# Planned times, queue order and output picking in a decoder kernel that attends over paged K/V

## The chip, the cores and the metric

The kernel runs on one core of a Trainium2 chip. The time is the device time of one execution in microseconds (us); lower is better. Three runs of the kernel before gave 2172.71, 2174.38 and 2177.74 us, median 2174.38 us.

## The reference

One inference step of a two-layer decoder, width 2048, for 256 prompt tokens and for 8 sequences of 8 new tokens that have 2048 past tokens each in a paged K/V cache. Layer A is an RWKV-7 recurrence. Layer B is stick-breaking attention with 16 heads of 128, on K and V that are projected once from the residual stream after layer A:

```python
k_p, v_p = _shared_kv(h_p, kv_norm, w_kv)              # prompt
k_past = cache_k[page_table].reshape(Bs, past_len, 16, 128)   # samples: 8 x 16 pages of 128
h_p = h_p + _sb_mix(rmsnorm(h_p), k_p, v_p, ...)       # causal, 256 x 256 per head
h_s = h_s + _sb_mix(rmsnorm(h_s), k_s_all, v_s_all, ...)
# in a block:  z = q.k * scale + bias;  att = exp(log_sigmoid(z) + sum of log_sigmoid(-z) over later keys)
# o = att @ v;  branch = (o * silu(g)) @ w_o,   q, g = split(rmsnorm(h) @ w_qg)
```

The outputs are the two y tensors, the states and shifts of layer A, and the new K and V.

## The kernel before, in words

Channels lie on the 128 partitions and tokens on the free axis: 320 tokens, 256 of the prompt and 64 of the samples. Every projection weight (2048 x 2048) is read in 16 chunks of 1 MB. A chunk is split into two parts of lower precision (`whi` by ScalarE, L1724, `wlo` by VectorE, L1898) and multiplied in three passes (L2100 to L2102). The program has an opening, mixing projections, the recurrence, and then the trunk (`trunk`), which this case is about.

The trunk computes six projections, 96 chunks: WO, Q, K, V, the gate G2, and BO at the end. Beside them run three kinds of work. **Sample attention** goes over 64 blocks (`NK`), each two pages of K and two of V of one sequence, 4 MB a block: scores (L2126), softplus and running sum, transposes (L2139), and the product with V (L2148), which adds up in `psO` over the 8 blocks of a sequence. **Prompt heads**, 16 of them, need the finished Q, K, V and G2 and read them back from DRAM (L1623 to L1625 and L1636, 128 KB each). **News** is the attention of each sequence to its own 8 new tokens, 8 times (L2185 to L2204), from `kN`, `vS`, `gS`. BO needs all heads and all sequences.

In `psO` the four output groups stand in 32-row lanes: of the 16 heads each is valid in a quarter of the rows. Before, ScalarE copies all 512 columns to SBUF (`osb`, L1800; `osn` for the news, L1841), TensorE multiplies the four 128-column parts with columns of the identity (`pick`, L2161 and L2204, 32 columns each), and VectorE stores them (L1987, L2027).

The order on every engine is fixed when the program is built. Each kind of work is a generator that yields a planned time before each step, and `side_by_side` (L567) always takes the step with the lowest planned time:

```python
CHUNK, SHARED = 7.0, 13.4
BLOCK = 12.0
WINDOW = 32 * CHUNK + GAP
SAMPLE = WINDOW + 8.0
HEADS, HEAD = WINDOW + 48 * SHARED + 4.0, 7.8
NEWS, NEWLY = HEADS + 4.0, 12.0
```

`SHARED` is the planned time of one of the 48 chunks of K, V and G2, during which the blocks run; `HEAD` and `NEWLY` are the planned times of a head and of a sequence's news. These numbers decide only the order; what an engine waits for is decided by semaphores. Block k is planned at `SAMPLE + 12 k` = 242 + 12 k. Put into the formulas, the heads began at 881.2, which is 53.3 blocks after the first one, and the news at 885.2; BO's first chunk is at 1031.6. SyncE's queue (SP) issues all loads of the trunk in one order. A load whose buffer isn't free yet holds up everything behind it: pages of K wait for the scores two blocks back (two buffers), pages of V for the value product three pages back (three buffers), Q, K and V of head h for head h-4, and the gate of head h for `p_y` of head h-6 (six buffers). PE starts the value product of a block (L2148) when both its V pages have landed.

Of the kernel before, what the change touches and what calls it, by code (L numbers as in the profile page):

```python
# [18 lines left out]
ALU = mybir.AluOpType  # L19
# [1333 lines left out]
AT_BIASQ, AT_BIAS, AT_MASK = 0, 2, 2 + NHB  # L1353
# [16 lines left out]
CHUNK, SHARED = 7.0, 13.4  # L1370
# [4 lines left out]
HEADS, HEAD = WINDOW + 48 * SHARED + 4.0, 7.8  # L1375
NEWS, NEWLY = HEADS + 4.0, 12.0
# [63 lines left out]
def trunk(nc, c_, a):  # L1440

    with ExitStack() as ctx:
# [11 lines left out]
        st, osb = sb("st", [P, 2, KB, P]), sb("osb", [P, 512])  # L1454
        pt = sb("pt", [1, NB * NPAGE], I32)
        biasQ = c_.consts[:, 3:4]
        pick = c_.ident[:].rearrange("p (g i q) -> p i g q", g=4, i=4)
        with ExitStack() as ring:
# [14 lines left out]
        er, osn = sb("er", [P, P]), sb("o_new", [P, 512])  # L1473
# [21 lines left out]
        att_turned, st_ready = sem("att_turned"), sem("st")  # L1495
# [4 lines left out]
                       (("t", "scored turned valued spread picked"), ("a", "abs exp ln att er st osn"),  # L1500
                        ("v", "z sp rc arg o gate")))
# [20 lines left out]
        def by_lane(x, b):  # L1522
            return x[:, :, TS * b:TS * b + TS].rearrange("p (g i) q -> p i g q", i=4)

        def lanes(x):
            return x.rearrange("p (i g q) -> p i g q", i=4, g=4)
# [19 lines left out]
        def _(sp):  # L1546
# [58 lines left out]
            def news():  # L1605
# [6 lines left out]
                yield HEADS + 16.0  # L1612
# [3 lines left out]
            def heads():  # L1616
                for h in range(NHB):
                    j = h % HRING
                    yield max(head_time(h - HRING, 0.4), low_time(first_chunk(BO) - 1) + 2.7)
# [7 lines left out]
            def gates():  # L1627
                for h in range(NHB):
                    yield max(head_time(h - GRING, 2.3), HEADS + 16.5 if h >= 4 * 3 else HEADS - 1.0)
# [11 lines left out]
            sp.dma_start(c_.consts[:, 2:4], a["at_fixed"][:, AT_BIASQ:AT_BIAS]).then_inc(fixed_in, 16)  # L1641
# [70 lines left out]
        def _(act):  # L1712
# [74 lines left out]
            def turned():  # L1787
                for k in range(NK):
# [19 lines left out]
            def news():  # L1808
# [7 lines left out]
                for b in range(NB):  # L1816
# [75 lines left out]
        def _(dve):  # L1892
# [110 lines left out]
            def news():  # L2003
                for b in range(NB):
# [17 lines left out]
                    Nv.done(dve.tensor_tensor(z_n[:], z_n[:], w_n[:], ALU.subtract), "arg")  # L2022
                    yield new_time(b, 0.86)
# [3 lines left out]
                    Nv.done(dve.tensor_tensor(by_lane(oN, b), lanes(pn_fin), by_lane(gS, b), ALU.mult), "o")  # L2027
                    Nv.wait(dve, "o", b)
                    g = of_sequence(gS, b)
                    Nv.done(dve.tensor_tensor(g, g, pn_er.rearrange("p (h q) -> p h q", q=TS), ALU.mult), "gate")  # L2030
# [48 lines left out]
        def _(pe):  # L2079
# [51 lines left out]
            def turns():  # L2131
                for k in range(NK):
# [20 lines left out]
                    if k % NBLK == NBLK - 1:  # L2153
# [6 lines left out]
                        for i in range(4):  # L2160
                            last = pe.matmul(ps_fin[:, 32 * i:32 * i + 32].rearrange("p (g q) -> p g q", g=4),  # L2161
                                             osb[:, i * P:(i + 1) * P], pick[:, i], start=True, stop=True)
                        last.then_inc(final_summed, 1)

            def news():
                yield NEWS - 5.0
# [8 lines left out]
                for b in range(NB):  # L2175
# [17 lines left out]
                    if b:  # L2193
                        Na.wait(pe, "osn", b - 1)
# [186 lines left out]
```

## Time and profile before

| what | value |
|---|---|
| median of three runs | 2174.38 us |
| the profiled execution: time, span | 2177.72 us, 2176.0 us |
| busy: PE, DVE, ACT, POOL | 89%, 46%, 38%, 12% |
| mean granted clock of TensorE | 0.951 of full speed |
| chain that ended last: PE, DMA | 27%, 20% of the span |
| the largest single item of that chain | landing of V pages, 20% |
| moved by DMA | 508.84 MB |

Times in the rows are microseconds from the start of the span. SPq is the DMA queue of SyncE. In a view by windows, the DMA share is the mean busy share of the core's 16 DMA engines, and PEclk is the granted clock as a share of the full 2.4 GHz. "Idle before, releaser" is the time in which an engine stood still ahead of an instruction, and what ended it.

### The profile page before, as it was taken

Reading aid. Unit: us, or ns where it says so; the run is one execution under the profiler, and the core shown is the slowest. Engines: PE = TensorE matmul, PEld = TensorE weight load, DVE = VectorE, ACT = ScalarE, POOL = GpSimd, SP = SyncE. Lnnn points to the kernel's source line nnn. Section 1 sums busy time; section 2 is a strip of 40 time slices with the busy share of each in tenths; the row PEclk is TensorE's granted clock in tenths of the full one; section 3 lists DMA queues with packets and bytes.
Section 4 is the critical chain, followed back from the end, with each engine's and each line's share of the span. In section 5 each row is a group of like instructions: output and inputs, shape, how many; then the busy total and the mean of one; then the engine's idle time right before and its main releaser. Section 6 shows DMA issues by size and latency. Waiting matters only on the chain.

```text
span 2176.0 us, 49310 instructions
## 1 busy us (share of the span) xinstructions
PE 1938.7 (89%) x20796; PEld 1652.4 (76%) x20796; DVE 993.1 (46%) x1551; ACT 822.9 (38%) x1430; POOL 261.6 (12%) x315
## 2 busy tenths in 40 slices
PE   5799999999799999969999988989988888687797
PEld 3599999999688888869899756656666666344596
DVE  6336364543455555424546433333353333366344
ACT  3523232332455555422323323233233334355332
POOL 2200000000244444313100000000000000010032
PEclk8899999999899999979999999999999999788898
DMA  5455555553222222144564999999999999988441
GB/s 189 155 166 162 176 159 179 168 170 101 76 80 67 74 72 69 46 168 147 222 218 163 419 419 419 418 418 414 410 403 416 419 419 378 343 321 333 157 151 68
DMA packets 119495, 508.84 MB, mean 234 GB/s; under 512 B 19233, under 2 KB 60578, under 8 KB 65826
## 3 DMA queue, kind: packets, MB, share of 16 engines
q1 hardware_dynamic: 119298, 506.00, 61.9%
q8 instruction: 149, 2.44, 0.5%
q14 instruction: 48, 0.39, 0.1%
HBM read 472.33 MB, written 33.63 MB: 233 GB/s over the span
## 4 chain that ended last, share of the span: by engine, by line
PE 27%; DMA 20%; DVE 3%; ACT 2%; SPq 2%; issue 2%; DVEq 0%; ACTq 0%
DMA at_vraw<-in_cache_v 20%; PE psP_ L2100 7%; PE psP_ L2101 6%; PE psP_ L2102 6%; PE at_psO L2148 4%; PE at_psS L2126 2%; DVE wlo_ L1898 1%; SPq L1551 1%; DMA at_gS<-spill_g 1%; DVE resT L2073 0%; SPq L1611 0%; ACT whi_ L1724 0%; ACT at_p_w L1856 0%; DMA wraw_<-in_weights 0%; PE psP_ L2196 0%
## 5 line engine op out<-in xcount | busy, mean ns | idle before, releaser
L2100 PE MATMUL psP_<-xhi,whi_ 128*128 128x320 f32 x1536 | 494.8, 322 | 24.6 <-DVE wlo_ L1898 14.8
L2101 PE MATMUL psP_<-xlo,whi_ 128*128 128x320 f32 x1536 | 478.7, 312 | 0.0
L2102 PE MATMUL psP_<-xhi,wlo_ 128*128 128x320 f32 x1536 | 478.4, 311 | 0.0
L2100 PEld LDWEIGHTS psP_<-xhi,whi_ 128*128 128x128 f32 x1536 | 292.6, 190 | 99.9 <-issue 83.7
L134 PE MATMUL psP<-xhi,whi 128*128 128x320 f32 x1024 | 318.0, 311 | 12.9 <-DVE wlo L169 11.9
L1898 DVE TENSOR_TENSOR wlo_<-wraw_,whi_ 128x2048 fp32r<-128x2048 f32 x96 | 222.1, 2314 | 210.0 <-ACT whi_ L1724 209.2
L135 PE MATMUL psP<-xlo,whi 128*128 128x320 f32 x1024 | 317.1, 310 | 0.0
L136 PE MATMUL psP<-xhi,wlo 128*128 128x320 f32 x1024 | 317.1, 310 | 0.0
L1724 ACT ACTIVATE whi_<-wraw_ 128x2048 fp32r<-128x2048 f32 x96 | 183.5, 1913 | 317.0 <-PE psP_ L2102 311.7
L2101 PEld LDWEIGHTS psP_<-xlo,whi_ 128*128 128x128 f32 x1536 | 293.1, 191 | 0.0
L2102 PEld LDWEIGHTS psP_<-xhi,wlo_ 128*128 128x128 f32 x1536 | 292.4, 190 | 0.0
L169 DVE TENSOR_TENSOR wlo<-wraw,whi 128x2048 fp32r<-128x2048 f32 x64 | 146.7, 2293 | 208.7 <-ACT whi L163 208.7
L2148 PE MATMUL at_psO<-at_vraw,at_st 128*32 128x512 f32 x1024 | 143.9, 686 | 86.1 <-DMA at_vraw<-in_cache_v 80.9
L163 ACT ACTIVATE whi<-wraw 128x2048 fp32r<-128x2048 f32 x64 | 122.3, 1913 | 240.8 <-PE psP L136 237.3
L134 PEld LDWEIGHTS psP<-xhi,whi 128*128 128x128 f32 x1024 | 193.0, 188 | 14.9 <-DVE wlo L169 13.2
L135 PEld LDWEIGHTS psP<-xlo,whi 128*128 128x128 f32 x1024 | 193.1, 189 | 0.0
L136 PEld LDWEIGHTS psP<-xhi,wlo 128*128 128x128 f32 x1024 | 193.0, 188 | 0.0
L2148 PEld LDWEIGHTS at_psO<-at_vraw,at_st 128*32 128x32 f32 x1024 | 29.4, 117 | 147.1 <-DMA at_vraw<-in_cache_v 92.3
L2126 PE MATMUL at_psS<-at_kraw,at_qp 128*32 128x256 f32 x2048 | 128.2, 392 | 0.0
L1793 ACT ACTIVATE at_st<-at_psT 128x256 f32<-128x256 f32 x64 | 24.5, 383 | 249.8 <-PE at_psT L2139 249.7
L2126 PEld LDWEIGHTS at_psS<-at_kraw,at_qp 128*32 128x32 f32 x2048 | 61.3, 112 | 48.1 <-issue 16.4
L1678 POOL COPY at_qp<-at_qS 128x128 f32<-128x128 f32 x8 | 3.2, 412 | 740.8 <-PE at_psS L2126 596.3
(315 smaller groups left out, 2721.7 us busy)
## 6 DMA issues: line engine op xcount, KB each, us to landing
at_kraw<-in_cache_k SPq DMA_DIRECT2D x128, 1024.0 KB, 11.1
at_vraw<-in_cache_v SPq DMA_DIRECT2D x128, 1024.0 KB, 10.9
wraw_<-in_weights SPq DMA_DIRECT2D x96, 1024.0 KB, 6.8
wraw<-in_weights SPq DMA_DIRECT2D x64, 1024.0 KB, 4.9
rw_s0t<-in_s0T SPq DMA_DIRECT2D x16, 256.0 KB, 3.7
o_wkv_s<-rw_SN SPq DMA_DIRECT2D x16, 256.0 KB, 2.3
resT<-in_xT SPq DMA_DIRECT2D x4, 640.0 KB, 5.9
spill_r<-stage SPq DMA_DIRECT2D x4, 640.0 KB, 7.4
```

Source lines behind the costliest of these rows:

```text
L134: pe.matmul(out, wh, c_.xhi[:, kc, :], start=(kc == 0), stop=False)
L135: pe.matmul(out, wh, c_.xlo[:, kc, :], start=False, stop=False)
L136: last = pe.matmul(out, wl, c_.xhi[:, kc, :], start=False, stop=(kc == NM - 1))
L163: act.activation(c_.whi[:, q % 2], c_.wraw[:, q], ACT.Copy).then_inc(c_.whi_ready, 1)
L169: dve.tensor_tensor(c_.wlo[:, q % 2], c_.wraw[:, q], c_.whi[:, q % 2], ALU.subtract).then_inc(c_.wlo_ready, 1)
L1724: act.activation(whi[:, i % 2], wraw[:, q], ACT.Copy).then_inc(c_.whi_ready, 1)
L1898: dve.tensor_tensor(wlo[:, i % 2], wraw[:, q], whi[:, i % 2], ALU.subtract).then_inc(c_.wlo_ready, 1)
L2100: pe.matmul(out, wh, c_.xhi[:, kc, :], start=(kc == 0), stop=False)
L2101: pe.matmul(out, wh, c_.xlo[:, kc, :], start=False, stop=False)
L2102: last = pe.matmul(out, wl, c_.xhi[:, kc, :], start=False, stop=(kc == NM - 1))
L2126: last = pe.matmul(psS[32 * j:32 * j + 32, 0:BK].rearrange("p (t s) -> p t s", t=KB), qp[:, b % 2, j, 32 * i:32 * i + 32], kraw[:, k % KRI ...
L2148: last = pe.matmul(psO[32 * g:32 * g + 32, :], st[:, k % 2, pg, 32 * g:32 * g + 32], vraw[:, (KB * k + pg) % VRING, 512 * g:512 * g + 512] ...
```

## The change

Four things change.

1. **Planned times.** `SHARED` 13.4 to 12.6, `HEAD` 7.8 to 9.6, `NEWLY` 12 to 14, and `NEWS` from `HEADS + 4` to `HEADS + 26`. The heads now begin at 842.8, 50.1 blocks after the first block, and the news at 868.8. The last block and BO keep their planned times.
2. **Queue of loads.** Q, K, V of head h are planned at `head_time(h, -2.6)` and no longer at `head_time(h - 4, 0.4)`; its gate at `head_time(h, -1.2)` and no longer at `head_time(h - 6, 2.3)`. `gS` moves from `HEADS + 16` to `HEADS + 22`.
3. **Picking of outputs.** The four 128-column parts of `psO` (and `psF`) are each multiplied by a 0/1 column of the partitions (`lane(i)`, loaded with the constants) and added up by VectorE in four dependent operations; one transpose on TensorE then gives the result. `osb` and `osn` shrink to 128 columns, ScalarE's copies are gone, and the four products with `pick` become one `transpose`. `oS` and `oN` are stored in plain head order.
4. With these, two waits change their engine: the wait for the last value product of a sequence goes from ScalarE to VectorE, and so does that of the news.

```diff
-AT_BIASQ, AT_BIAS, AT_MASK = 0, 2, 2 + NHB
+AT_BIASQ, AT_LANES, AT_BIAS, AT_MASK = 0, 1, 5, 5 + NHB
-CHUNK, SHARED = 7.0, 13.4
+CHUNK, SHARED = 7.0, 12.6
-HEADS, HEAD = WINDOW + 48 * SHARED + 4.0, 7.8
-NEWS, NEWLY = HEADS + 4.0, 12.0
+HEADS, HEAD = WINDOW + 48 * SHARED + 4.0, 9.6
+NEWS, NEWLY = HEADS + 26.0, 14.0
...
-                yield HEADS + 16.0
+                yield HEADS + 22.0
                 sp.wait_ge(c_.stored, spilled_before(BO))
                 sp.dma_start(gS[:], sample_part("g2")).then_inc(gs_in, 16)
...
-                    yield max(head_time(h - HRING, 0.4), low_time(first_chunk(BO) - 1) + 2.7)
+                    yield max(head_time(h, -2.6), low_time(first_chunk(BO) - 1) + 2.7)
...
-                    yield max(head_time(h - GRING, 2.3), HEADS + 16.5 if h >= 4 * 3 else HEADS - 1.0)
+                    yield max(head_time(h, -1.2), HEADS + 22.0 if h >= 4 * 3 else HEADS - 1.0)
...
-                    if k % NBLK == NBLK - 1:
-                        b = k // NBLK
-                        yield block_time(k, 1.9)
-                        act.wait_ge(valued, KB * (k + 1))
-                        if b:
-                            act.wait_ge(final_summed, b)
-                        act.activation(osb[:], psO[:], ACT.Copy).then_inc(o_copied, 1)
...
-                    yield new_time(b, 0.68)
-                    Nt.wait(act, "valued", b)
-                    if b:
-                        Nt.wait(act, "picked", b - 1)
-                    Na.done(act.activation(osn[:], psF, ACT.Copy), "osn")
...
             def finals():
                 for b in range(NB):
+                    yield block_time(NBLK * b + NBLK - 1, 1.9)
+                    dve.wait_ge(valued, KB * NBLK * (b + 1))
+                    if b:
+                        dve.wait_ge(final_summed, b)
+                    dve.tensor_scalar(osb[:], psO[:, 0:DH], lane(0), None, ALU.mult).then_inc(laned, 1)
+                    for i in range(1, 4):
+                        dve.wait_ge(laned, 3 * b + i)
+                        dve.scalar_tensor_tensor(out=osb[:], in0=psO[:, DH * i:DH * i + DH], scalar=lane(i), in1=osb[:],
+                                                 op0=ALU.mult, op1=ALU.add).then_inc(laned if i < 3 else o_copied, 1)
                     yield block_time(NBLK * b + NBLK - 1, 2.25)
                     dve.wait_ge(final_summed, b + 1)
-                    dve.tensor_copy(by_lane(oS, b), lanes(ps_fin)).then_inc(final_out, 1)
+                    dve.tensor_copy(of_sequence(oS, b), by_head(ps_fin)).then_inc(final_out, 1)
...
+                    yield new_time(b, 0.68)
+                    Nt.wait(dve, "valued", b)
+                    if b:
+                        Nt.wait(dve, "picked", b - 1)
+                    Nv.done(dve.tensor_scalar(osn[:], psF[:, 0:DH], lane(0), None, ALU.mult), "l0")
+                    for i in range(1, 4):
+                        Nv.wait(dve, f"l{i - 1}", b)
+                        Nv.done(dve.scalar_tensor_tensor(out=osn[:], in0=psF[:, DH * i:DH * i + DH], scalar=lane(i),
+                                                         in1=osn[:], op0=ALU.mult, op1=ALU.add), f"l{i}")
...
-                        for i in range(4):
-                            last = pe.matmul(ps_fin[:, 32 * i:32 * i + 32].rearrange("p (g q) -> p g q", g=4),
-                                             osb[:, i * P:(i + 1) * P], pick[:, i], start=True, stop=True)
-                        last.then_inc(final_summed, 1)
+                        pe.transpose(ps_fin, osb[:], c_.ident[:]).then_inc(final_summed, 1)
...
-                        last = pe.matmul(pn_fin[:, 32 * i:32 * i + 32].rearrange("p (g q) -> p g q", g=4),
-                                         osn[:, i * P:(i + 1) * P], pick[:, i], start=True, stop=True)
-                    Nt.done(last, "picked")
+                    Nv.wait(pe, "l3", b)
+                    Nt.done(pe.transpose(pn_fin, osn[:], c_.ident[:]), "picked")
```

## Rows read from the trace of the kernel before

**Rows 1.** Windows of the trunk: length, busy per engine (instructions), PEclk, DMA share, GB/s.

```profile
core 0: us, PE busy (x) PEld busy (x) DVE busy (x) ACT busy (x) POOL busy (x), PEclk, DMA share, GB/s
1196.60:1840.00 643.40, 571.85 (x4822) 415.97 (x4824) 242.91 (x321) 213.90 (x350) 2.71 (x6) 0.97 1.01 413
1840.00:1860.00 20.00, 13.38 (x114) 8.20 (x106) 4.26 (x9) 6.92 (x16) 2.22 (x3) 0.83 1.01 395
1860.00:1897.00 37.00, 20.06 (x193) 11.64 (x194) 11.69 (x28) 13.18 (x34) 2.79 (x5) 0.75 0.89 329
1897.00:2017.00 120.00, 95.93 (x928) 55.59 (x931) 74.99 (x183) 70.64 (x187) 11.47 (x18) 0.87 0.88 329
2017.00:2032.00 15.00, 9.26 (x80) 5.27 (x76) 6.63 (x15) 6.88 (x17) 0.00 (x0) 0.84 0.61 233
```

**Rows 2.** The chain that ended last, two of its steps between 1200 and 1840 us.

```profile
1229.22 10.86 DMA at_vraw<-in_cache_v
1240.13 1.11 PE at_psO L2148 x8
```

**Rows 3.** Waits, 1196.6 to 1840 us: engine, line, releaser, total, times, longest.

```profile
PE at_psO L2148 <- DMA at_vraw<-in_cache_v: 69.5, 36, 4.4
DVE at_oS L1987 <- PE at_psM L2161: 22.7, 5, 11.3
```

**Rows 4.** Waits of SyncE's DMA queue, 1840 to 2040 us.

```profile
SPq L1551 <- PE at_psO L2148: 46.4, 12, 8.7
SPq L1636 <- DVE at_p_y L2061: 39.9, 8, 13.1
SPq L1561 <- DVE at_p_z L2040: 8.4, 1, 8.4
SPq L1622 <- PE psP_ L2229: 7.1, 7, 3.4
```

**Rows 5.** SyncE's queue around the hole: start, time, line, what it issues.

```profile
1881.11 0.33 SPq L1575 DMA_DIRECT2D at_vraw<-in_cache_v  x1
1881.49 0.43 SPq L1614 DMA_DIRECT2D at_gS<-spill_g  x1
1895.05 0.33 SPq L1636 DMA_DIRECT2D at_p_g<-spill_g  x1
1895.88 0.34 SPq L1575 DMA_DIRECT2D at_vraw<-in_cache_v  x1
```

**Rows 6.** VectorE in time order: scores of blocks 53 and 63, and the hole.

```profile
1858.71 0.47 DVE L1971 TENSOR_SCALAR at_z<-at_psS,consts 128x256 f32<-128x256 f32 x1
...
1892.49 0.29 DVE L2027 TENSOR_TENSOR at_oN<-psP_,at_gS 128x128 f32<-128x128 f32 x1 [17.63 <-DMA at_gS<-spill_g]
...
1894.61 0.42 DVE L2061 TENSOR_TENSOR at_p_y<-psP_,at_p_g 128x256 f32<-128x256 f32 x1
...
2020.67 0.47 DVE L1971 TENSOR_SCALAR at_z<-at_psS,consts 128x256 f32<-128x256 f32 x1
```

**Rows 7.** DMA issues, 1897 to 2017 us: count, KB each, median us to landing.

```profile
at_vraw<-in_cache_v SPq DMA_DIRECT2D x16, 1024.0 KB, 7.0
at_kraw<-in_cache_k SPq DMA_DIRECT2D x14, 1024.0 KB, 7.1
wraw_<-in_weights SPq DMA_DIRECT2D x2, 1024.0 KB, 10.3
at_p_k<-o_kk SPq DMA_DIRECT2D x10, 128.0 KB, 3.9
at_p_v<-o_kv SPq DMA_DIRECT2D x10, 128.0 KB, 3.8
at_p_g<-spill_g SPq DMA_DIRECT2D x9, 128.0 KB, 4.9
at_p_q<-spill_q SPq DMA_DIRECT2D x9, 128.0 KB, 3.9
```

**Rows 8.** One line's or tile's instructions: duration ns min/median/max, first and last start.

```profile
L1800 ACT ACTIVATE at_osb<-at_psO x8: 575/582/599, 1295.1 to 2035.6; 128x512 f32<-128x512 f32 x8
L2027 DVE TENSOR_TENSOR at_oN<-psP_,at_gS x8: 280/292/292, 1892.5 to 1996.5; 128x128 f32<-128x128 f32 x8
L2190 PE MATMUL psP_<-ident,at_z_new x8: 272/298/422, 1870.0 to 1992.9; 128*64 128x128 f32 x8
```

**Rows 9.** The end of the trunk's middle part, PE, DVE and ACT, in time order.

```profile
2031.93 3.61 PE L2148 MATMUL at_psO<-at_vraw,at_st 128*32 128x512 f32 x16 [1.98 <-DMA at_vraw<-in_cache_v]
2036.26 1.08 PE L2161 MATMUL at_psM<-ident,at_osb 128*128 128x32 f32 x8 [0.73 <-ACT at_osb L1800]
...
2038.04 2.29 DVE L1898 TENSOR_TENSOR wlo_<-wraw_,whi_ 128x2048 fp32r<-128x2048 f32 x1 [6.91 <-ACT whi_ L1724]
2040.25 0.28 DVE L1987 COPY at_oS<-at_psM 128x128 f32<-128x128 f32 x1
2040.45 2.28 DVE L1898 TENSOR_TENSOR wlo_<-wraw_,whi_ 128x2048 fp32r<-128x2048 f32 x1
2042.65 0.28 DVE L1995 TENSOR_TENSOR at_oS<-at_oS,at_gS 128x128 f32<-128x128 f32 x1
2042.97 0.29 DVE L1997 TENSOR_TENSOR at_oS<-at_oS,at_oN 128x128 f32<-128x128 f32 x1
2043.63 0.29 DVE L2000 TENSOR_TENSOR xlo<-at_oS,xhi 128x128 fp32r<-128x128 f32 x1 [0.37 <-ACT xhi L1806]
...
2029.99 0.38 ACT L1793 ACTIVATE at_st<-at_psT 128x256 f32<-128x256 f32 x1 [1.86 <-PE at_psT L2139]
...
2035.61 0.60 ACT L1800 ACTIVATE at_osb<-at_psO 128x512 f32<-128x512 f32 x1 [4.94 <-PE at_psO L2148]
2036.11 3.70 ACT L1724 ACTIVATE whi_<-wraw_ 128x2048 fp32r<-128x2048 f32 x2
```

**Rows 10.** The chain that ended last: BO's first product after the middle part.

```profile
2044.21 0.61 PE psP_ L2100
```

More of the change, by code:

```diff
@@ L1453, in trunk @@
         z, w = (sb(x, [P, 2, BK]) for x in ("z", "w"))
-        st, osb = sb("st", [P, 2, KB, P]), sb("osb", [P, 512])
+        st, osb = sb("st", [P, 2, KB, P]), sb("osb", [P, DH])
         pt = sb("pt", [1, NB * NPAGE], I32)
         biasQ = c_.consts[:, 3:4]
-        pick = c_.ident[:].rearrange("p (g i q) -> p i g q", g=4, i=4)
         with ExitStack() as ring:
@@ L1472, in trunk @@
         qn, st_n = sb("qn", [P, 2, 4, 160]), sb("st_new", [NEW, P])
-        er, osn = sb("er", [P, P]), sb("o_new", [P, 512])
+        er, osn = sb("er", [P, P]), sb("o_new", [P, DH])
         zp = [sb(f"p_z{j}", [P, ZW]) for j in range(3)]
@@ L1494, in trunk @@
         rc_ready, arg_ready, att_ready = (sem(x) for x in ("rc", "arg", "att"))
-        att_turned, st_ready = sem("att_turned"), sem("st")
+        att_turned, st_ready, laned = sem("att_turned"), sem("st"), sem("laned")
         o_copied, final_summed, final_out = sem("o_copied"), sem("final_summed"), sem("final_out")
@@ L1499, in trunk @@
         Nt, Na, Nv = (Marks(sem("new_" + x), names.split()) for x, names in
-                       (("t", "scored turned valued spread picked"), ("a", "abs exp ln att er st osn"),
-                        ("v", "z sp rc arg o gate")))
+                       (("t", "scored turned valued spread picked"), ("a", "abs exp ln att er st"),
+                        ("v", "z sp rc arg l0 l1 l2 l3 o gate")))
         p_q_in, p_k_in, p_v_in = ([sem(f"p_{x}_in{j}") for j in range(HRING)] for x in "qkv")
@@ L1520, in times, with lane, by_head @@
             return 16 * (h // HRING + 1)
[L1522 to L1526, printed above, removed]
+        def lane(i):
+            return c_.consts[:, 4 + i:5 + i]
+        def by_head(x):
+            return x.rearrange("p (h q) -> p h q", q=TS)
         def of_sequence(x, b):
@@ L1640, in _ @@
             sp.dma_start(pt[:], a["page_table"].rearrange("(o b) n -> o (b n)", o=1)).then_inc(pt_in, 16)
-            sp.dma_start(c_.consts[:, 2:4], a["at_fixed"][:, AT_BIASQ:AT_BIAS]).then_inc(fixed_in, 16)
+            sp.dma_start(c_.consts[:, 3:8], a["at_fixed"][:, AT_BIASQ:AT_BIAS]).then_inc(fixed_in, 16)
             sp.wait_ge(pt_in, 16)
@@ L2026, in news @@
                         dve.wait_ge(gs_in, 16)
-                    Nv.done(dve.tensor_tensor(by_lane(oN, b), lanes(pn_fin), by_lane(gS, b), ALU.mult), "o")
+                    Nv.done(dve.tensor_tensor(of_sequence(oN, b), by_head(pn_fin), of_sequence(gS, b), ALU.mult), "o")
                     Nv.wait(dve, "o", b)
                     g = of_sequence(gS, b)
-                    Nv.done(dve.tensor_tensor(g, g, pn_er.rearrange("p (h q) -> p h q", q=TS), ALU.mult), "gate")
+                    Nv.done(dve.tensor_tensor(g, g, by_head(pn_er), ALU.mult), "gate")
             def heads():
@@ L2193, in news @@
                     if b:
-                        Na.wait(pe, "osn", b - 1)
+                        Nv.wait(pe, "l3", b - 1)
                     for g in range(4):
@@ L2201, in news @@
                     yield new_time(b, 0.78)
-                    Na.wait(pe, "osn", b)
-                    for i in range(4):
-                        last = pe.matmul(pn_fin[:, 32 * i:32 * i + 32].rearrange("p (g q) -> p g q", g=4),
-                                         osn[:, i * P:(i + 1) * P], pick[:, i], start=True, stop=True)
-                    Nt.done(last, "picked")
+                    Nv.wait(pe, "l3", b)
+                    Nt.done(pe.transpose(pn_fin, osn[:], c_.ident[:]), "picked")
             def heads():
@@ L2273, in program @@
         c_.ones = sb("ones", [P, P])
-        c_.consts = sb("consts", [P, 4])
+        c_.consts = sb("consts", [P, 8])
         c_.vec = sb("vec", [P, NM * len(VECS)])
@@ L2344, in laid_out @@
     new[:, NEW - TS:NEW] = np.where(np.arange(TS) < q[:, None] % TS, 0.0, MASKED)
-    out["at_fixed"] = np.concatenate([np.repeat(bias, 2 * TS).reshape(P, 2), np.broadcast_to(bias, (P, NHB)), *causal, new],
+    lanes = (q[:, None] // TS % 4 == np.arange(4)).astype(bias.dtype)
+    out["at_fixed"] = np.concatenate([np.repeat(bias, TS)[:, None], lanes, np.broadcast_to(bias, (P, NHB)), *causal, new],
                                      axis=1).astype(bias.dtype)
```

## The prediction

> **What bounds the kernel now.** Read first the chain that ended last and the busy shares in slices: PE is busy nearly everywhere, but from 1197 us on V pages join the chain. Then read the trunk in windows [rows 1]. Between 1196.6 and 1840 us the DMA share is 1.01 at 413 GB/s: the pages and weights fill the link, and this stage, which I call the shared stage, is transfer-bound. Its chain shows the same [rows 2]: a V page lands 10.9 us after its issue, and PE takes 1.1 us for the half block that frees the next buffer. PE is idle for 643.4 - 571.9 = 71.5 us there, and 69.5 us of PE's waits there name V pages [rows 3]; so PE would have room.
>
> Then the link stops being full. In the last 192 us before the last value product (1840 to 2032 us, the tail) the DMA share is 1.01, 0.89, 0.88 and 0.61 in the four windows [rows 1]. Idle link time: 37 x 0.11 + 120 x 0.12 + 15 x 0.39 = 4.1 + 14.4 + 5.9 = 24.4 us. PE isn't full either (139 of 192 us), nor DVE (98 of 192). So nothing is used up in the tail; it goes by waits in queues. The queue view names them [rows 4]: SyncE's queue stood 39.9 us for the gate buffers (`p_y`), 13.1 us at worst, 8.4 us for the BO weights and 7.1 us for head buffers. All page loads are behind that. The worst case can be read in order [rows 5, 6]: gS is issued at 1881.5; the gate load behind it waits for p_y; VectorE waits 17.6 us for gS to land, and p_y stands behind that same wait on VectorE; the next V page is only issued at 1895.9, though the queue had issued one at 1881.1. From the planned times this is built in: the consumer of gS was planned at NEWS + 0.86 x 12 = HEADS + 14.3, its load at HEADS + 16.
>
> **The planned times.** The 48 chunks now take 604.8 planned units, not 643.2, so 604.8/12 = 50.4 blocks stand beside them instead of 53.6: 3.2 blocks, 12.8 pages of 1.05 MB, 13.4 MB, 32 us at 418 GB/s, leave the shared stage and go to the tail. No byte is added or removed. Per chunk the link must carry 1.05 MB of weights, 0.16 MB of spill and (12.6/12) x 4.19 = 4.40 MB of pages, 5.61 MB, against 5.89 before; a chunk took 643.4/48 = 13.4 us, and should take 13.4 x 5.61/5.89 = 12.75 us. PE's busy time per chunk is 571.9/48 = 11.9 us before and about 11.6 after (a block costs it about 4.4 us: 1.9 scores, 1.9 values, 0.6 transposes, an estimate), so the link stays the bound, with 1.1 us of room per chunk.
>
> As pure exchange between stages that is 0. What it is worth is the filling of the tail. There a head's four loads cost the link more than their bytes: between 1897 and 2017 us, 32 loads of 1 MB take 32 x 1.05/0.418 = 80.3 us of the 105.6 us of busy link (120 x 0.88), and 38 loads of 128 KB the other 25.3 us, 0.67 us each, 2.7 us a head [rows 1, 7]. With HEAD = 7.8 there are 1.54 heads for a block of 10.0 us of pages; with 9.6 there are 1.25. The link's need per block becomes 10.0 + 1.25 x 2.7 = 13.4 us. PE's work per block of the tail was 95.9 us over the 8.2 blocks that the window holds (16.2 us a block from block 53 to 63, 14.6 without the hole) = 11.6 us [rows 1, 6], and falls by 0.29 heads of 3.4 us and 0.14 news of 3.5 us to about 10.1 us (estimates from the timeline's durations). Pages so come to be ahead of the arithmetic, and the link can run nearly without holes.
>
> **The queue.** Before, the gate load of head h stood 0.2 heads behind the p_y that frees its buffer, 1.6 us; now it stands at h - 1.2 against h - 6 + 2.1 = h - 3.9, 2.7 heads or 26 units later. Q, K and V are at h - 2.6 against h - 3.75, 1.15 heads or 11 units, where they had 0.15 heads (1.2). So the 39.9 and 7.1 us of queue waits go, except what real lag leaves. Still early enough: 25 units ahead of use for Q and K, 32 for gates, against landings of 3.8 to 4.9 us [rows 7]. gS is loaded at HEADS + 22 and used at HEADS + 38: the 17.6 us hole goes. BO's third and fourth chunk move ahead of three V pages instead of one; their wait for the last head's scores is planned 2.6 units behind those, and the bytes are the same: 0. What is late next is the V buffer loop itself, in which the queue stood 46.4 us [rows 4]; it can't be filled at the very end, where the last V page may only be issued after the block before it.
>
> Of the 24.4 us idle I take 10 to remain: about 6 at the end, as now (15 x 0.39), and 4 spread over the rest. **-14 us.** Bounds: 3 remaining (-21) and 22 (-2), the latter if waits just move.
>
> **Picking.** Before: 0.58 us on ACT, then PE 1.08 us. After: four VectorE operations that read PSUM and wait for each other. A 128x128 operation with a PSUM source takes 0.29 us [rows 8], and two dependent ones start 0.32 us apart [rows 9]: 4 x 0.32 = 1.3 us; then one transpose, 0.3 us [rows 8]. 16 such picks: ACT loses 9 us, PE about 12 us, DVE gains 20 us, none of it from a full engine. During the shared stage PE and DVE time is covered by the link (rows 1); if that cover were gone, 7 x 1.3 us. The new wait on VectorE for the last value product has the evacuations, the splits and the next block's softplus behind it. But VectorE already waited at that place, for the pick [rows 3], 22.7 us in 5 times; it now waits 0.35 blocks earlier for work that ends at the same time: 0, bounds 0 to 7 x 2 us if the link runs dry. In the news the same holds: the new wait stands 1.1 units behind the product, 8 times: 0 to +6, inside the bounds of the tail.
>
> **The end.** After the last value product the row of steps is now [rows 9]: end of PE 2035.54, ACT copies 0.6, then both BO splits (3.7) and both low parts on VectorE (2.3, 2.3) in which oS and the sums stand, and BO starts at 2044.21 [rows 10], 8.7 us later. ACT's split was behind the copy, which waited 4.9 us for the product. In the new plan the splits stand at 1014.6, right behind the last `st`, with nothing to wait for, so they and the low parts run during the wait for the last V page. From the last st (2029.99) they end 0.4 + 3.7 + 2.3 = 6.4 us later, now 2036.4, 0.9 us after the product. Then four picks 1.3, transpose and its hops 0.7, store 0.3, sums, high and low part 1.3, PE's start 0.3: 3.9 us. BO starts about 4.8 us after the product, not 8.7: **-4 us**, bounds -5 to -1 (-1 if the page lands early).
>
> **Sum.** -14 - 4 = -18 us against the profiled 2177.7 us (span 2176.0), 2159.7. That execution lies 3.3 us above the median of 2174.4, so 2156 us.
>
> **Rivals.** (a) *The tail goes by its chains of dependent steps, not by loads.* For: no engine is full; PE's clock is 0.84 to 0.87 [rows 1]. Then 14.6 us a block minus 0.29 heads of arithmetic, about 13.8 us, instead of 13.4; over 13 blocks +5, and the holes at both ends stay (+6): 2167 us. Against: the largest waits are the queue's, and they have named releasers. (b) *The tail is already full for its mix of loads*, idle shares being gaps between small packets, so only the end gains: 2170 us. For: 329 GB/s both in the window with the hole and in that without it. Against: the hole shows nothing issued for 13 us. The Trainium skill, page Perfetto Trace Analysis, section What "DMA-bound" means, says that for a kernel bound by DMA engines or their sequencer large descriptors are what matters; this change makes none larger. Its page DMA: Bandwidth & Descriptors, section Specifications, gives about 358 GB/s as the HBM limit of a core; by it the tail's 63 MB would need 176 of the 192 us, which leaves 16 to win. The trace disagrees, with 413 GB/s over 643 us [rows 1]. (c) *Slower: the shared stage stops being transfer-bound.* 12.75 us per chunk leave PE 1.1 us; if fixed waits on PE, ACT and the moved VectorE wait need more than that, the chunk stays at 13.4 us, and 48 x 0.65 = 31 us come on top, while the tail still carries its 3.2 blocks: 2187 us. It decides from 1.1 us of unhidden waits per chunk; the waits of PE there that don't name V pages are about 2 us in the whole stage [rows 1, 3]. (d) *The change doesn't do what it says*: real lag puts heads so late that the queue meets the same waits, and the lanes wait eats the end: 2174 us.
>
> **Numbers.** Forecast 0.64, with a better outcome down to 2148 in it; (a) 0.15; (b) 0.07; (c) 0.09; (d) 0.05. 0.2% (4.3 us) is about what a measurement can tell from no change. Faster: forecast, (a) and two thirds of (b), 0.84; same: a third of (b) and most of (d), 0.06; slower 0.10. Range: forecast with remaining idle 3 and end -5 gives -26, 2148; two more for what the median may move, 2146; upward (a) and (b), 2170.
>
> **What would show it.** Right: no VectorE wait for gS; queue waits for p_y under 5 us; the shared stage shorter by about 30 us at a DMA share of 1.0; DMA share of at least 0.95 from there to the last V page; BO's first product within 5.5 us of the last value product, with whi splits ahead of it. Wrong: DMA share under 0.98 in the shared stage (rival c); queue waits gone but the share still 0.88 (a, b); new waits on VectorE for value products of over 10 us in the tail.

## The result: 1.3% faster, about 29 us

The changed kernel runs in 2144.66 us, median of 4 runs (2142.77 to 2147.81), beside 2173.55 us for the kernel before (4 runs, 2169.48 to 2177.74): ratio 0.9868, 95% interval 0.9845 to 0.9891. I had predicted 2156 us, a gain of 18 us, and a range that began at 2146. The sign was right. The size was more than a third too small, and the time lies 1.3 us outside the range.

The profiled execution of the changed kernel took 2142.77 us with a span of 2141.1 us, 34.9 us less than the one before. 4.8 us of that stand ahead of the first scores of block 0, which start at 1188.7 us and not at 1193.5; that part differs by 3.3 us between two runs of the full change. So I count from the first scores. From there to BO's first product it is 820.9 us, against 850.7 before: 29.8 us less.

The first view is by windows, cut at four marks: first scores of block 0, first scores of head 0 (VectorE's `at_p_z`), the same of head 15, the last value product, BO's first product. The changed kernel:

```profile
core 0: us, PE busy (x) PEld busy (x) DVE busy (x) ACT busy (x) POOL busy (x), PEclk, DMA share, GB/s
1188.70:1820.80 632.10, 563.52 (x4757) 414.85 (x4756) 250.60 (x345) 213.94 (x347) 4.71 (x8) 0.97 1.01 412
1820.80:1976.40 155.60, 113.54 (x1185) 57.85 (x1183) 102.01 (x256) 81.84 (x221) 14.55 (x23) 0.91 1.00 390
1976.40:2000.80 24.40, 11.08 (x92) 4.88 (x93) 8.60 (x19) 10.17 (x23) 0.00 (x0) 0.84 0.85 345
2000.80:2009.60 8.80, 3.70 (x18) 0.81 (x18) 6.97 (x10) 2.51 (x3) 0.00 (x0) 0.69 0.57 209
```

And the kernel before, cut at the same marks (new windows, which cut the time of [rows 1] elsewhere):

```profile
1193.50:1862.90 669.40, 590.09 (x4965) 428.94 (x4964) 248.75 (x335) 225.11 (x372) 4.93 (x9) 0.96 1.01 412
1862.90:2020.20 157.30, 117.42 (x1134) 67.38 (x1133) 86.78 (x212) 82.40 (x217) 14.26 (x22) 0.84 0.87 323
2020.20:2031.90 11.70, 5.99 (x40) 3.39 (x38) 6.53 (x14) 6.56 (x16) 0.00 (x0) 0.86 0.71 269
2031.90:2044.20 12.30, 4.68 (x24) 1.58 (x25) 5.48 (x6) 4.50 (x4) 0.00 (x0) 0.64 0.24 76
```

Stage by stage: -37.3, -1.7, +12.7 and -3.5 us. The shared stage lost four blocks (VectorE starts the scores of 50 blocks in it, before 54). **The heads' stretch took three of them in and was as long as before**: VectorE starts the scores of twelve blocks (50 to 61) in it now, of nine (54 to 62) before, in 155.6 and 157.3 us. (Counted by PE's products it is 12 and 10 blocks, because block 63 stood right at the old border.) Two blocks are left behind the last head, and the end is shorter. The stretch now runs the link at 1.00, where it was at 0.87. Its granted clock is 0.91, where it was 0.84.

The queue of SyncE between 1800 and 2020 us answers to [rows 4]:

```profile
SPq L1551 <- PE at_psO L2154: 52.7, 15, 14.2
SPq L1551 <- PE at_psS L2132: 38.5, 10, 8.8
SPq L1562 <- DVE wlo_ L1886: 9.1, 2, 7.3
SPq L1561 <- PE psP_ L2229: 3.6, 1, 3.6
SPq L1636 <- DVE at_p_y L2067: 0.4, 1, 0.4
```

The 39.9 us for `p_y` became 0.4 us, and the 7.1 us for head buffers are gone. Most of what is left waits for page buffers, and that grew: 91.2 us, where it was 51.2 (46.4 and 4.8 us, 1840 to 2040 us). VectorE doesn't wait for gS any more [rows 6]: the load is issued at 1845.4 and takes 11.9 us, and its first use comes at 1870.8.

The end, in place of [rows 9] (VectorE, then ScalarE, then PE):

```profile
1998.75 0.42 DVE L2070 TENSOR_TENSOR xlo<-at_p_y,xhi 128x256 fp32r<-128x256 f32 x1 [0.48 <-ACT xhi L1863]
2001.23 4.49 DVE L1886 TENSOR_TENSOR wlo_<-wraw_,whi_ 128x2048 fp32r<-128x2048 f32 x2 [2.06 <-ACT whi_ L1724]
2005.64 0.34 DVE L1977 TENSOR_SCALAR at_osb<-at_psO,consts 128x128 f32<-128x128 f32 x1
2006.02 1.12 DVE L1980 SCALAR_TENSOR_TENSOR at_osb<-at_psO,consts,at_osb 128x128 f32<-128x128 f32 x3
...
1999.29 3.71 ACT L1724 ACTIVATE whi_<-wraw_ 128x2048 fp32r<-128x2048 f32 x2 [0.30 <-DVE xlo L2070]
...
1993.49 3.46 PE L2154 MATMUL at_psO<-at_vraw,at_st 128*32 128x512 f32 x16 [8.39 <-DMA at_vraw<-in_cache_v]
2000.79 3.22 PE L2154 MATMUL at_psO<-at_vraw,at_st 128*32 128x512 f32 x16 [2.76 <-DMA at_vraw<-in_cache_v]
2007.20 0.47 PE L2166 MATMUL at_psM<-ident,at_osb 128*128 128x128 f32 x1 [3.19 <-DVE at_osb L1980]
2009.58 0.60 PE L2106 MATMUL psP_<-xhi,whi_ 128*128 128x320 f32 x1 [1.90 <-DVE xlo L1997]
```

The splits now run beside the last value product. They begin only at 1999.3, behind the last head's low part (1998.75), and PE did that head's product behind a value product that stood 8.4 us for a V page. So VectorE's lanes wait 1.6 us for the second split, and BO starts 5.6 us after the product's end (2004.0), not 4.8 and not 8.7.

### The profile page after: what moved, and what is told of

It is laid out like the page before. It is cut to its first block, busy times and chain, and to the rows that moved or that the text cites. A ratio compares the mean times of both kernels' runs of the same rounds, so it can differ in the third digit from the quotient of the medians.

```text
span 2141.1 us, 49135 instructions
## 1 busy us (share of the span) xinstructions
PE 1913.5 (89%) x20684; PEld 1630.1 (76%) x20684; DVE 1013.3 (47%) x1615; ACT 813.2 (38%) x1414; POOL 263.8 (12%) x315
## 4 chain that ended last, share of the span: by engine, by line
PE 29%; DMA 18%; DVE 4%; ACT 2%; SPq 2%; issue 2%; DVEq 0%; ACTq 0%
DMA at_vraw<-in_cache_v 17%; PE psP_ L2106 7%; PE psP_ L2108 7%; PE psP_ L2107 7%; PE at_psO L2154 4%; PE at_psS L2132 2%; DVE wlo_ L1886 1%; SPq L1551 1%; PE psP_ L2199 0%; DVE resT L2079 0%; SPq L1611 0%; ACT whi_ L1724 0%; DVE at_xtmp L1922 0%; ACT xhi L1768 0%; DMA wraw_<-in_weights 0%
## 5 line engine op out<-in xcount | busy, mean ns | idle before, releaser
L134 PE MATMUL psP<-xhi,whi 128*128 128x320 f32 x1024 | 317.8, 310 | 12.5 <-DVE wlo L169 11.9
L134 PEld LDWEIGHTS psP<-xhi,whi 128*128 128x128 f32 x1024 | 192.9, 188 | 14.5 <-DVE wlo L169 13.2
L1793 ACT ACTIVATE at_st<-at_psT 128x256 f32<-128x256 f32 x64 | 24.4, 382 | 263.4 <-PE at_psT L2145 263.4
```

The source lines that it names most:

```text
L134: pe.matmul(out, wh, c_.xhi[:, kc, :], start=(kc == 0), stop=False)
```

## The experiments

The times "from the first scores" below are those of the profiled executions, counted as above, since the part ahead of the first scores varies by some microseconds from run to run. A ratio compares with the kernel before on the same chip, whose median lay between 2173.55 and 2179.88 us; so medians of different experiments are compared by their ratios.

### Which part of the change brings it

**Times and queue, without the picking.** The change's numbers and load positions in the kernel before:

```diff
-CHUNK, SHARED = 7.0, 13.4
+CHUNK, SHARED = 7.0, 12.6
-HEADS, HEAD = WINDOW + 48 * SHARED + 4.0, 7.8
-NEWS, NEWLY = HEADS + 4.0, 12.0
+HEADS, HEAD = WINDOW + 48 * SHARED + 4.0, 9.6
+NEWS, NEWLY = HEADS + 26.0, 14.0
...
+                    yield max(head_time(h, -2.6), low_time(first_chunk(BO) - 1) + 2.7)
+                    yield max(head_time(h, -1.2), HEADS + 22.0 if h >= 4 * 3 else HEADS - 1.0)
```

> Planned times and queue positions of the change, outputs picked as before. My theory (the gain is the link's idle time in the tail, refilled; picking is worth only the hops at the end): about 24 to 27 us faster than before, within 5 us of the full change; SyncE's queue waits under 2 us for p_y; VectorE doesn't wait for gS. The splits of BO stand before ScalarE's last copy here too, by their planned time, so most of the shorter end stays. Rival (the shorter news chain and less work on PE and ACT let the tail follow the link): at most 12 us faster, DMA share in the tail under 0.95.

Measured: 2152.52 us, ratio 0.9871 (0.9855 to 0.9886). From the first scores to BO 824.4 us, 26.3 less than before.

**The picking alone**, all numbers and positions as before.

> Only the picking by VectorE with 0/1 columns and one transpose; planned times and queue positions as before. My theory: the 17.6 us wait for gS and the waits for p_y stay; 0 to 3 us faster, from the end alone (the BO splits stand right before the lanes' operations, with no copy on ScalarE that they wait behind). Rival: 12 us or more faster.

Measured: 2176.36 us, ratio 0.9986 (0.9973 to 0.9999), from the first scores 848.5 us, 2.2 less. VectorE waits 15.4 us for gS and the queue 49.0 us for p_y there. So 26 of the 30 us come without the picking, and it brings 2.2 us alone and 3.5 us on top of the rest, by single profiles; the ratios of the full change and of this run without picking (0.9868 and 0.9871) can't be told apart.

**All but the queue positions.** The full change with the loads of heads, gates and gS planned as before:

```diff
-                    yield max(head_time(h, -2.6), low_time(first_chunk(BO) - 1) + 2.7)
+                    yield max(head_time(h - HRING, 0.4), low_time(first_chunk(BO) - 1) + 2.7)
-                    yield max(head_time(h, -1.2), HEADS + 22.0 if h >= 4 * 3 else HEADS - 1.0)
+                    yield max(head_time(h - GRING, 2.3), HEADS + 16.5 if h >= 4 * 3 else HEADS - 1.0)
```

> The full change without its queue positions: Q, K, V of head h again at head h-4 + 0.4, gates at h-6 + 2.3, gS at HEADS + 16 (now 22 units before its use, as the news start later). My theory: the gS hole is gone by the later news, but the gate loads again wait for p_y and hold up pages: 5 to 15 us slower than the full change, p_y waits of 15 to 40 us in SyncE's queue. Rival (the planned times do it all): within 3 us of the full change.

Measured: 2150.72 us, ratio 0.9863 (0.9848 to 0.9878), which can't be told from the full change. In the profile it is 826.3 us from the first scores, 5.4 more than the full change. The queue does wait 22.9 us for p_y again, as I expected, but it costs 0 to 5 us. I had expected 5 to 15 us: by the ratio a miss, and by the profile the low edge. **The planned times do most of it, and most of the time that the queue stands is not time of the kernel**.

**The hole alone.** One number in the kernel before:

```diff
-                yield HEADS + 16.0
+                yield HEADS + 2.0
                 sp.wait_ge(c_.stored, spilled_before(BO))
                 sp.dma_start(gS[:], sample_part("g2")).then_inc(gs_in, 16)
```

> The kernel before with one edit: gS is loaded at HEADS + 2 and no longer at HEADS + 16, so that it lands before its first use. Theory (the one built-in hole is a large part): VectorE's 17.6 us wait and the 13.1 us gate wait go, 8 to 15 us faster. Rival (the hole is only a place where lag is paid that is paid elsewhere otherwise): under 4 us.

Measured: 2172.62 us, ratio 0.9961 (0.9950 to 0.9973), from the first scores 843.1 us, 7.6 less. The wait for gS fell from 17.6 to 1.6 us. Its size in the time is at the low edge of what I expected, about half of the wait that disappeared. (Starting the news ten units later in the kernel before, `NEWS = HEADS + 14.0`, would be a second way to remove the hole. In that order the engines wait for each other without end, so it has no time.)

**The gain in three parts.** From the first scores to BO it is 850.7 us before, 843.1 without the hole, 824.4 with times and queue as well, and 820.9 with the picking: 7.6, 18.7 and 3.5 us, taken in this order. The heads' stretch without the hole (nine blocks, by VectorE's scores), and with times and queue (twelve), both with the old picking:

```profile
1858.40:2010.80 152.40, 119.35 (x1134) 68.65 (x1133) 86.47 (x212) 82.49 (x217) 14.28 (x22) 0.83 0.89 332
1824.40:1985.80 161.40, 124.98 (x1248) 68.12 (x1246) 91.45 (x221) 86.23 (x230) 14.59 (x23) 0.87 0.97 376
```

So the three blocks aren't free there: the stretch is 9.0 us longer, 3.0 us a block, where each of the four blocks had 9.3 us in the shared stage (37.3/4). The full change has the same length as the kernel before because two other things make room: the hole is gone (157.3 to 152.4 us), and the picking is lighter (161.4 to 155.6 us). These are pairs of single profiles, and the order of the steps alone moves the stretch by 8 us and more (below), so 3.0 us a block is an estimate. One more thing may count: the granted clock of the stretch is 0.83 and 0.84 in the two kernels with nine blocks, 0.87 and 0.91 in the two with twelve. No run holds the clock fixed, so its share stays open.

### What holds the heads' stretch

**The loads of heads left out.** The changed kernel, and the kernel before, without 46 of the 64 loads of 128 KB. What is left out: heads 4 to 15 work on Q, K and V of earlier heads, and gates of heads 6 to 15 are those of earlier ones. The engines wait for the first load of a buffer alone; the queue's own waits for these buffers stay in both kernels.

```diff
+                    if h >= HRING:
+                        continue
                     sp.dma_start(Q[j][:], c_.spill[SP_I["q"]][h][:, 0:SEQ]).then_inc(p_q_in[j], 16)
...
+                    if h >= GRING:
+                        continue
                     sp.dma_start(G[h % GRING][:], c_.spill[SP_I["g2"]][h][:, 0:SEQ]).then_inc(p_g_in[h % GRING], 16)
```

> The changed kernel without 46 of its 64 loads of 128 KB: Q, K, V of heads 4 to 15 and the gates of heads 6 to 15 are left out, and the heads work on what the buffers hold, so the heads' outputs are others. Every instruction of the engines stays. Theory (the tail of the changed kernel is bound by the link, and a small load costs it 0.38 us there): 46 x 0.38 = 17 us faster than the full change (about 2127 us by its first median). By the price that I read from the kernel before, 0.67 us, it would be 31 us. Rival (the tail goes by chains of dependent steps): under 5 us.

Measured: 2148.61 us, ratio 0.9857 (0.9833 to 0.9880): nothing that can be told from the full change. The window of its heads' stretch has the same length with a link that is less full:

```profile
1826.80:1982.60 155.80, 113.48 (x1185) 57.85 (x1183) 102.05 (x256) 81.85 (x221) 14.57 (x23) 0.91 0.92 351
```

In the kernel before:

> The kernel before without the same 46 loads (heads 4 to 15 work on what the buffers hold, gates of heads 6 to 15 too); the waits of SyncE's queue for p_scored, p_vturned and p_y go with the loads. Theory (the tail of the kernel before is held by its order, with 1.54 heads per block and the gS hole, which stays): 5 to 12 us faster than before, less than in the changed kernel. Rival (transfer-bound like the other): 17 us or more. If the queue's 39.9 us of p_y waits were what held the tail: 20 us or more as well, with a DMA share near 1.

Measured: 2172.98 us, ratio 0.9978 (0.9965 to 0.9992), about 5 us; from the first scores 847.5 us, 3.2 less. The expectation was wrong on the edit: the waits didn't go with the loads. The queue stands 34.3 us for head buffers and 17.5 us for p_y, and VectorE 14.1 us for gS. So this run says what the loads cost, and nothing on the queue's waits. The stretch takes 154.4 us:

```profile
1861.00:2015.40 154.40, 115.92 (x1134) 66.34 (x1133) 87.06 (x212) 82.06 (x217) 14.28 (x22) 0.86 0.77 288
```

My theory for the first of the two fell: the heads' stretch of the changed kernel is not bound by the link, though its share is 1.00.

**Pages left out.** The changed kernel without the page loads of blocks 52 to 63, the kernel before without those of blocks 56 to 63; the blocks work on the pages that lie in the buffers.

```diff
             def load_key(k, pg):
+                if k >= 52:
+                    return
...
-                    pe.wait_ge(k_in[k % 2], 32 * (k // 2 + 1))
+                    pe.wait_ge(k_in[k % 2], min(32 * (k // 2 + 1), 832))
```

(and the same for V; 56 and 896 in the kernel before).

> The changed kernel without the page loads of blocks 52 to 63 (48 of 256 loads of 1 MB): these blocks work on the pages that lie in the buffers, and SyncE's queue doesn't wait for their buffers. All instructions of the engines stay. Theory (the heads' stretch is held by chains of dependent steps over PE, ScalarE and VectorE, in the planned order, not by transfers): the 15 heads' distance from first to last score stays within 8 us of the 155.6 us of the full change, and only PE's waits for V pages near both ends go (some 25 us at most): 10 to 25 us faster in all. Rival (transfers, by bandwidth or by the buffer loop, hold it): 40 us or more faster, the heads' distance under 135 us.

Measured: 2126.61 us, ratio 0.9769 (0.9754 to 0.9784), from the first scores 804.7 us, 16.2 less than the full change.

```profile
1821.70:1970.80 149.10, 110.56 (x1185) 56.85 (x1183) 102.51 (x257) 81.92 (x221) 14.45 (x23) 0.93 0.34 111
```

With less than a third of the transfers (111 against 390 GB/s) the stretch is 6.5 us shorter. The other 10 us lie behind the last head: from there to BO it is 23.5 us, not 33.2. In the changed kernel PE waits 12.4 us for V pages there, here not at all.

> The kernel before without the page loads of blocks 56 to 63 (32 loads of 1 MB), in the same way. Theory of chains: the distance of the 15 heads stays within 8 us of 157.3 us, less the part of the gS hole that was due to the queue's wait for pages (up to 10 us more); 5 to 20 us faster in all. Rival of transfers: 25 us or more.

Measured: 2170.84 us, ratio 0.9977 (0.9965 to 0.9988), the stretch 151.3 us at a DMA share of 0.35. So in both kernels it is mainly the arithmetic in its planned order that holds this stretch: 149 us and 151 us with most of the link empty, beside twelve and nine blocks. In the second of them VectorE still waits 13.2 us for gS, and the queue 69.5 us for p_y, so its 151 us aren't arithmetic alone.

The chain of the middle of the stretch shows it in both traces. For the changed kernel between 1880 and 1960 us, and for the kernel before between 1900 and 1980 us, its shares by line (the view cuts its rows at the right):

```profile
by line: issue 12.9%; PE at_psS L2132 7.5%; PE psP_ L2199 6.6%; DVE at_o_new L2027 6.0%; DVE at_p_rc L2055 4.4%; DVE at_w L1965 3.7%; DVE at_p_w L2050 3.6%; DVE at_p_rc L2053 3.2%; ACT at_p_w L1844 2.7%; ACT at_p_w L1842 2.5%; PE at_psO L21
```

```profile
by line: issue 13.2%; PE at_psS L2126 6.8%; PE psP_ L2196 4.8%; PE at_psO L2148 4.5%; ACT at_p_w L1856 3.3%; DVE at_p_rc L2049 3.0%; DVE at_w L1977 2.8%; ACT at_p_w L1854 2.8%; PE psP_ L2221 2.7%; PE psP_ L2229 2.7%; DVE at_p_w L2044 2.4%; 
```

No landing of a page is among the largest items there, where V pages are 61% of the chain of the shared stage before (1196 to 1860 us). The time goes mostly in steps of 0.3 to 3.6 us on PE, ScalarE and VectorE. This could be read before the change. Near the two ends of the stretch it is different. Over the whole of it (1820.8 to 1976.4 us) V pages are the largest single item of the chain, 11.4%, in two landings:

```profile
1830.18 10.67 DMA at_vraw<-in_cache_v
1971.33 7.15 DMA at_vraw<-in_cache_v
```

Before, V pages are 7.6% of the whole stretch and gS is 6.9%. The run without pages prices the first kernel's landings at no more than the 6.5 us above.

**Heads not further apart.** The full change with HEAD 7.8 and NEWLY 12:

```diff
-HEADS, HEAD = WINDOW + 48 * SHARED + 4.0, 9.6
-NEWS, NEWLY = HEADS + 26.0, 14.0
+HEADS, HEAD = WINDOW + 48 * SHARED + 4.0, 7.8
+NEWS, NEWLY = HEADS + 26.0, 12.0
```

> The changed kernel with HEAD and NEWLY as before (7.8 and 12): the projections are closer, the heads aren't further apart. 1.54 heads again stand beside a block, and some 4 blocks are left alone behind the last head. Theory of chains: the 15 heads take as long as in the other kernels, 150 to 157 us, and the 4 blocks behind them come on top at 10 to 12 us each: 20 to 40 us slower than the full change, close to the kernel before. Rival (the shorter shared stage gives the gain whatever the heads do): within 5 us of the full change.

Measured: 2168.65 us, ratio 0.9962 (0.9948 to 0.9975), by the ratios 20 us slower than the full change; from the first scores 847.0 us, 26.1 more.

```profile
1822.50:1979.20 156.70, 114.42 (x1074) 59.30 (x1076) 98.68 (x246) 79.44 (x212) 14.56 (x23) 0.85 0.89 342
1979.20:2029.90 50.70, 23.28 (x210) 9.17 (x203) 17.66 (x31) 16.07 (x32) 0.00 (x0) 0.72 0.87 352
```

The heads take 156.7 us, though 117 units were planned for 15 of them and not 144. The blocks that don't stand beside them come afterwards, 50.7 us instead of 24.4. Four blocks' scores start behind the last head, not two. So closer projections alone bring little: the gain needs the heads planned so far apart that the blocks stand beside them.

### The order of loads at the end

**BO's weights later.** I had put BO's third and fourth chunk ahead of the last V pages at 0, "the bytes are the same". In the full change, planned behind them:

```diff
     if first + 2 <= i < first + 4:
-        return head_time(NHB - 1, 0.5) + 0.1 * (i - first)
+        return block_time(NK - 1, 0.7) + 0.1 * (i - first)
```

> The changed kernel with BO's third and fourth chunk loaded after the last V page instead of before the last three. Theory (in a full link, order is time: 2.1 MB ahead of the last pages cost 2.1/0.418 = 5 us): 3 to 5 us faster than the full change, the last value product that much earlier. Rival (as I put it in the prediction, same bytes, 0; or BO then waits for its third chunk): within 1 us.

> The full change with BO's chunks three and four behind the last V page, once more: 5 to 7 us faster than the full change (its BO began 6.8 us earlier, counted from the first scores), ratio to before 0.981 to 0.985.

Measured: 2136.31 us, ratio 0.9812 (0.9793 to 0.9831), and again, beside a repeat of the full change on the same chip, 2139.41 us, ratio 0.9823 (0.9802 to 0.9844).

> The full change once more, for direct comparison with the late BO weights and with the steps beside it on the same chip: 0.986 to 0.988 of the time before.

The repeat of the full change: 2147.08 us, ratio 0.9868 (0.9845 to 0.9891), from the first scores 819.8 us. So the later weights bring 7.7 us in the medians of that comparison. In the profiles BO's first product comes 814.1 and 813.5 us after the first scores, 5.7 and 6.3 us less than in the repeat. The last value products no longer stand 8.4 us in one place:

```profile
1984.49 1.92 PE L2154 MATMUL at_psO<-at_vraw,at_st 128*32 128x512 f32 x16 [0.98 <-DMA at_vraw<-in_cache_v]
1994.44 1.92 PE L2154 MATMUL at_psO<-at_vraw,at_st 128*32 128x512 f32 x16 [3.10 <-DMA at_vraw<-in_cache_v]
2000.97 3.64 PE L2154 MATMUL at_psO<-at_vraw,at_st 128*32 128x512 f32 x16 [3.53 <-DMA at_vraw<-in_cache_v]
```

This is the fastest of the complete kernels here: about 1.8% faster than before.

### Further in the same direction

All three have the late weights too.

```diff
-CHUNK, SHARED = 7.0, 12.6
+CHUNK, SHARED = 7.0, 12.4
-HEADS, HEAD = WINDOW + 48 * SHARED + 4.0, 9.6
+HEADS, HEAD = WINDOW + 48 * SHARED + 4.0, 9.9
```

> The changed kernel with late BO weights (chunks three and four behind the last V page) and one step further in the same direction: SHARED 12.4, HEAD 9.9. 0.8 blocks more go from the shared stage to the heads. Theory of chains: as long as the link isn't full beside the heads, a block moved there is nearly free, so 3 to 9 us faster than the kernel with late weights alone. Rival (the link is full there now, its share being 1.02 to 1.03): a block costs 12 us in one place as in the other, within 2 us.

Measured: 2147.84 us, ratio 0.9862 (0.9847 to 0.9877): slower than late weights alone, by 0.4 to 0.5% of the time. A miss. The heads' stretch was 166.6 us long, 11 more.

With SHARED 12.6 and HEAD 9.2:

> Late BO weights and HEAD 9.2 instead of 9.6, with SHARED 12.6. If the distance of the heads is what the further step (SHARED 12.4, HEAD 9.9) made worse, this goes the other way or is equal: the 15 heads take 150 to 156 us, and the last head ends before the last pages, within 3 us of late weights alone. If the heads' length follows the order without a rule, 5 us or more off in either direction.

Measured: 2147.38 us, ratio 0.9866 (0.9844 to 0.9889); the stretch 163.4 us.

With SHARED 12.4 and HEAD 9.6:

> Late BO weights, SHARED 12.4 and HEAD 9.6. It differs from the slower further step only in HEAD (9.9 there) and from late weights alone only in SHARED. If the heads' distance was the cause there, this is 3 to 9 us faster than late weights alone; if the 0.8 blocks more beside the heads were (link full), it is 0 to 4 us off; if neither number but the order that they happen to give, it can be slower by 5 us or more with a heads' distance above 160 us.

Measured: 2145.34 us, ratio 0.9860 (0.9837 to 0.9882); the stretch 155.7 us. It begins 4.9 us earlier than with late weights alone (627.0 against 631.9 us after the first scores), but the pages are then behind: the last value product starts 811.7 us after the first scores, 6 us later.

So neither the planned distance of the heads nor the blocks beside them fixes the length by a rule. With 117 to 148.5 planned units it was 152 to 167 us in these kernels, 163.4 at HEAD 9.2 and 155.7 at 9.6, with the same instructions. What differs by the edits is which step stands before which in each engine's order. Which of these steps cost the 8 to 11 us stays open.

## Why the prediction was right or wrong

**What bounds the shared stage: right.** The DMA share is 1.01 at 412 GB/s in both kernels. It became 37.3 us shorter where I had 32, because it moves 15.4 MB less (275.8 to 260.4 MB, its length times 412 GB/s) and not 13.4: four blocks' scores fewer stand ahead of head 0, and not 3.2. Rival (c), a shared stage that isn't transfer-bound any more, didn't come.

**The step that failed is the ledger of the tail.** I took the link's idle time in the tail, 24.4 us, as the store from which the gain comes, assumed that it must also carry 3.2 more blocks at 10.0 us each, and let 10 us of idle time remain: -14. In truth the last value product came 26.4 us earlier (838.4 to 812.1 us from the first scores). Two things were wrong in it. First, the link's cost of a head's loads, 2.7 us or 0.67 us a load, was what the busy share left over when the pages were counted at 418 GB/s. The kernels without 46 of these loads measure it: busy link in the heads' stretch fell from 136.9 to 118.9 us in the kernel before (157.3 x 0.87 and 154.4 x 0.77), 0.39 us a load, and from 155.6 to 143.3 us in the changed one (155.8 x 0.92), 0.27 us. These are estimates, since the shares have two digits. For 64 loads my sum had 18 to 26 us as filled that were free.

Second, and more important, a ledger of the link was the wrong account for this stage. Idle link time was neither what the tail lacked nor what the gain was taken from: with the link at 0.92 instead of 1.00 the changed kernel's stretch is as long, and at 0.34 it is 6.5 us shorter. It is held mainly by its dependent steps, at 10 to 11 us a head in all kernels here. A block between them costs about 3 us, an estimate from the two runs with the old picking, not its 10.0 us of link nor the 13.4 us that I gave a block. So the account that fits is: the shared stage gets 37.3 us shorter, the stretch stays about as it was (three blocks in, hole and heavy picking out), 12.7 us more lie behind it, and the end is 3.5 us shorter.

**Rival (a) had the mechanism and the wrong unit.** "The tail goes by its chains of dependent steps" was right. But I priced it per block (13.8 us over 13 blocks, 2167 us), as if each block brought its own time. The stretch follows the heads much more than the blocks, which lie mostly in its gaps. Taken so, this rival would have given a larger gain than my forecast and not a smaller one. It had 0.15.

**The queue: waits right, worth wrong.** The waits for p_y and for head buffers went as the planned distances said, from 39.9 to 0.4 us and from 7.1 to 0. But with 22.9 us of them back the time was the same by the ratios, and 5.4 us longer in the profile. A queue that waits for a buffer costs something only if the load behind it lands too late. The hole of gS was real, and worth 8 us of its 17.6.

**Picking: right.** Four VectorE operations with 0.38 us from one start to the next (2005.64 to 2006.02), 1.5 us where I had 1.3, and a transpose of 0.3 us (median of 8; 0.47 us at the end). Alone it gave 2.2 us in the profile. In the news VectorE waits 10.6 us in 5 times for the value product. By my own list, over 10 us of such waits was a sign of being wrong, but it was no good sign: ScalarE had 10.3 us at the same place before. What I had at 0 was the work that picking saves in the heads' stretch: with it the stretch is 5.8 us shorter (161.4 to 155.6 us), of which 3.5 us are left at BO.

**The end: right in mechanism, -3.1 us instead of -4.** The splits did move beside the product, held up by the last head. BO began 5.6 us after it; my sign for being right was 5.5.

**BO's weights: wrong.** "The same bytes, 0" cost 6 to 8 us. At this stage's end it matters which bytes come first.

**The range.** Its lower end, 2146 us, stood for an idle link of 3 us, in the same ledger with the same overpriced loads. That the measured time came so close to it is luck: it is made of other terms. Rival (b), a tail full for its mix of loads, is refuted twice, by 390 GB/s over 155.6 us with the same loads and by the kernels without them.

## What to carry to other kernels

When two kinds of work share engines in one planned order, find for each stage what it keeps when the other is thinned out, and price the moved work in each by its own measure. Here a block took 9.3 us in the shared stage, which goes by megabytes, and some 3 us beside the heads (an estimate), whose stretch goes by dependent steps. Look for this in the chain of waits of exactly that stretch, its ends included: where landings are a small part of it, idle link time isn't the account to add up. And when the order is made from planned times, look at the last loads ahead of a barrier, and move behind them what is needed only after it.

## What the runs showed of the hardware

A DMA share of 1.00 doesn't say that transfers bound a stretch: 46 loads less changed the share from 1.00 to 0.92 and the length from 155.6 to 155.8 us, and 48 page loads less changed them to 0.34 and 149.1 us. A load of 128 KB in rows of 1 KB took 0.27 to 0.39 us of busy link, an estimate from the two kernels without 46 of them; its bytes at 418 GB/s are 0.31 us. And the part of the program ahead of the first scores ended between 1188.7 and 1197.7 us in these profiles, a spread larger than several of the effects here; the marks inside the trunk repeated within 1 to 2 us (820.9 and 819.8 us for the full change).
